# The second MLP's sample product by seven quadrant products, chunks 1 to 14, and retention states loaded in the other parity

## The reference

```
h = _rms_norm(x, norm_mlp[i]) * (1.0 + sc2) + sh2
x = x + g2 * (jnp.square(jax.nn.relu(h @ mlp_w1[i])) @ mlp_w2[i])
```

## Time and profile before

| | us |
|---|---|
| median of 3 runs | 2645.57 |
| lowest and highest run | 2644.88, 2650.03 |
| profiled execution | 2645.16 |
| its span | 2643.4 |
| TensorE (matmul) busy | 2561.9 (97%) |
| VectorE busy | 1351.4 (51%) |
| ScalarE busy | 593.9 (22%) |
| GpSimd busy | 544.8 (21%) |

### The profile page before, as it was taken

The page is one execution under the profiler, slowest core; times in us unless marked ns, Lnnn a source line. Parts: engine busy times, 40 slices in busy tenths (PEclk is TensorE's granted clock), DMA queues, the critical chain, the costliest instruction groups (busy, mean ns, idle before and its releaser), DMA issues.

```text
span 2643.4 us, 37530 instructions
## 1 busy us (share of the span) xinstructions
PE 2561.9 (97%) x14604; PEld 2240.7 (85%) x14604; DVE 1351.4 (51%) x2366; ACT 593.9 (22%) x982; POOL 544.8 (21%) x230
## 2 busy tenths in 40 slices
PE   7899999979999999999999999999999999999998
PEld 3878899977888888888888888888888888888887
DVE  6635752264385556554556555564444444444445
ACT  3311122142231111111111112751112111121112
POOL 6124321162121212111112111011121211212110
PEclk9999999989999999999999999899999999999999
DMA  7314523274212211211211211011010100101102
GB/s 236 149 67 142 166 96 112 95 265 168 72 33 80 71 56 56 95 56 56 71 56 56 95 56 32 25 32 33 32 48 32 48 32 32 48 32 48 32 32 80
DMA packets 126263, 199.48 MB, mean 75 GB/s; under 512 B 4420, under 2 KB 102504, under 8 KB 125800
## 3 DMA queue, kind: packets, MB, share of 16 engines
q1 hardware_dynamic: 123216, 188.76, 21.1%
q10 hardware_dynamic: 2968, 9.63, 1.2%
HBM read 167.44 MB, written 26.74 MB: 73 GB/s over the span
## 4 chain that ended last, share of the span: by engine, by line
PE 88%; DVE 5%; issue 2%; DMA 2%; ACT 2%; POOL 1%; ACTq 0%; SPq 0%; DVEq 0%; POOLq 0%
PE bank L314 83%; PE bank L1404 1%; PE bank L1432 1%; PE bank L1557 1%; DMA ada_st_in<-in_ada_w_dram 1%; PE bank L1469 1%; DVE ada_acc_in L1053 0%; PE bank L1735 0%; DVE vtok L1107 0%; DMA SB<-state_spill 0%; DVE xgm L1220 0%; POOL ringL L854 0%; DVE h1L L1227 0%; DVE X L1061 0%; ACT pF L736 0%
## 5 line engine op out<-in xcount | busy, mean ns | idle before, releaser
L854 POOL TENSOR_TENSOR ringL<-stage,ringH 128x2048 fp32r<-128x2048 f32 x82 | 392.8, 4790 | 1823.1 <-ACT ringH L532 1823.1
L1061 DVE SCALAR_TENSOR_TENSOR X<-bank,mod,X 128x512 f32<-128x512 f32 (+1 forms) x792 | 515.1, 660 | 363.4 <-PE bank L314 359.1
L314 PE MATMUL bank<-midH,ringH 128*128 128x512 f32 (+1 forms) x1536 | 546.7, 356 | 3.3 <-DVE X L1061 3.3
L314 PE MATMUL bank<-midL,ringH 128*128 128x512 f32 (+1 forms) x1536 | 544.9, 355 | 0.0
L314 PE MATMUL bank<-midH,ringL 128*128 128x512 f32 (+1 forms) x1536 | 544.7, 355 | 0.0
L314 PE MATMUL bank<-hH,ringH 128*128 128x512 f32 (+1 forms) x1248 | 447.2, 358 | 0.2 <-DVE hL L1227 0.2
L314 PE MATMUL bank<-hH,ringL 128*128 128x512 f32 (+1 forms) x1248 | 442.5, 355 | 0.0
L314 PE MATMUL bank<-hL,ringH 128*128 128x512 f32 (+1 forms) x1248 | 442.4, 355 | 0.0
L1336 DVE TENSOR_TENSOR relu<-relu 128x512 f32<-128x512 f32 (+1 forms) x192 | 146.3, 763 | 568.9 <-ACT relu L774 568.8
L774 ACT ACTIVATE relu<-bank 128x512 f32<-128x512 f32 (+1 forms) x192 | 100.9, 527 | 1375.9 <-PE bank L314 1375.9
L314 PEld LDWEIGHTS bank<-midH,ringH 128*128 128x128 f32 x1536 | 291.5, 190 | 46.1 <-DVE X L1061 6.5
(11 more groups left out here) (191 smaller groups left out, 2888.1 us busy)
## 6 DMA issues: line engine op xcount, KB each, us to landing
stage<-in_mlp_w_dram SPq DMA_DIRECT2D x64, 1024.0 KB, 5.3
ada_st_mlp<-in_ada_w_dram SPq DMA_DIRECT2D x18, 1536.0 KB, 8.3
stage<-in_ev_w_in_dram SPq DMA_DIRECT2D x14, 1024.0 KB, 5.1
ada_st_in<-in_ada_w_dram SPq DMA_DIRECT2D x8, 1536.0 KB, 9.5
ada<-in_ada_w_dram SPq DMA_DIRECT2D x8, 1024.0 KB, 13.3
x_spill<-X SPq DMA_DIRECT2D x1, 5120.0 KB, 18.5
gate_spill<-gate_st ACTq DMA_DIRECT2D x8, 640.0 KB, 3.7
gt<-gate_spill SPq DMA_DIRECT2D x20, 256.0 KB, 3.3
```

Of the source, the lines that this page charges most:

```text
L314: mm = nc.tensor.matmul(out, a, b, start=first and n == 0, stop=last and n == 2)
L854: nc.gpsimd.tensor_tensor(ringL[slot][:, :], stage[:, :], ringH[slot][:, :].bitcast(F32), ALU.subtract).then_inc(w_lo, 1)
L1061: V.scalar_tensor_tensor(out=X[:, d, cols(t)], in0=src[:, 0:TB[t][1]], scalar=gate_ap, in1=X[:, d, cols(t)], op0=ALU.mult, op1=ALU.add).th ...
```

## The change

In the second MLP the chunks 1 to 14 run a new function `mlp_fast` on each engine. The prompt's block keeps its products. The sample tokens' second product is cut into two halves of the output (four tiles each), two halves of the hidden units (one tile each) and two blocks of tokens, and the eight quadrant products are replaced by seven (Winograd's form of Strassen's scheme). Four of them use a sum of weight quadrants (S1 to S4, made by GpSimd in float32, split as the units are) or a sum of hidden quadrants (T1 to T4, made by VectorE). A quadrant product is four products of three matmuls, one for each output tile, and each is evicted on its own. Some add to a bank that was evicted before and holds its value (`CHAIN`).

The order on TensorE: first products 0, 1, 2; the quadrants 1 and 2 (8 products); first products 3, 4, 5; the quadrants 6, 5, 7, 3, 4, two output tiles at a time (20 products); 8 products of the prompt. The squares of the first products 3 to 5 go to ScalarE. The lowerings of the prompt's two hidden tiles (`p0`, `p1`) stand on VectorE behind the evictions of products 11 and 13.

```diff
+FAST_SEQ = ([(1, d) for d in range(HD)] + [(2, d) for d in range(HD)]
+            + [(p, d) for d0 in range(0, HD, 2) for p in (6, 5, 7, 3, 4) for d in (d0, d0 + 1)] + [("prompt", d) for d in range(DT)])
+FAST_BANK = [(2, 3, 6, 1, 4, 5, 2, 3)[d] if p == "prompt" else (6, 1)[d % 2] if p in (2, 3, 5) else 2 + d for p, d in FAST_SEQ]
...
+            def second_product(n):
+                own = earlier(FAST_BANK, n)
+                pe.wait_ge(m2_ev[l], p0 + own + 1)
+                pe.wait_ge(mid_lo[l], h0 + LO_ORDER.index(m_name) + 1)
...
+                pair_pass(bank[FAST_BANK[n]][:, :], wH, wL, mH, mL, p not in CHAIN, True, chained=True).then_inc(m2_mm[l], 1)
```

VectorE's part:

```diff
+            square(0)
+            lower("B11", b11)
...
+            square(1)
+            lower("B21", b21)
+            square(2)
+            dve.wait_ge(sqr_ok[l], n0 + 3)
+            V.tensor_tensor(t1, b12, b11, ALU.subtract).then_inc(t_full[l], 1)
+            for n in range(2 * HD):
+                evict(n)
...
+            V.tensor_tensor(t2, b22, t1, ALU.subtract).then_inc(t_full[l], 1)
+            V.tensor_tensor(t3, b22, b12, ALU.subtract).then_inc(t_full[l], 1)
+            dve.wait_ge(t_full[l], 4 * ch - 2)
+            V.tensor_tensor(t4, b21, t2, ALU.subtract).then_inc(t_full[l], 1)
+            lower("T1")
+            dve.wait_ge(t_full[l], 4 * ch)
+            lower("T2")
+            lower("T3")
+            lower("B22")
+            lower("T4")
+            for n in range(2 * HD, FAST_GRP):
+                evict(n)
+                if n in (11, 13):
+                    lower("p0" if n == 11 else "p1")
```

The end of ScalarE's part, and GpSimd's:

```diff
+            relu(5, hidden("p1")[2])
+            square(5, hidden("p1")[2])
+            act.wait_ge(sqr_ok[l], n0 + 6)
+            high("p1")
+            split_hi(U + 2, (m1_mm[l], n0 + PAIRS), U_MLP[l] % 2)
...
+            nc.gpsimd.tensor_tensor(s1, a21, a22, ALU.add).then_inc(s_add[l], 1)
+            nc.gpsimd.tensor_tensor(s3, a11, a21, ALU.subtract).then_inc(s_add[l], 1)
...
+            split_lo(U + 1, (U_MLP[l] + 1) % 2)
+            pool.wait_ge(s_hi[l], ch)
+            pool.wait_ge(t_full[l], 4 * ch - 3)
+            nc.gpsimd.tensor_tensor(sumL[:, :, :], sumF[:, :, :], sumH[:, :, :].bitcast(F32), ALU.subtract).then_inc(s_lo[l], 1)
+            split_lo(U + 2, U_MLP[l] % 2)
```

The states of block `k` go to `S[d][(k + 1) % 2]`, so that the first load does not overwrite the final states; SP's wait for the input products moves behind the loads:

```diff
-        sp.wait_ge(in_mm, IN_CUM[N_IN])
...
-                sp.dma_start(S[d][k % 2][:, :, :].rearrange("p h e -> p (h e)"), s_dram[d][k]).then_inc(s_back[k % 2], 16)
+                sp.dma_start(S[d][(k + 1) % 2][:, :, :].rearrange("p h e -> p (h e)"), s_dram[d][k]).then_inc(s_back[k % 2], 16)
...
         state_loads(0)
+        for d in range(2):
+            sp.dma_start(new_state[0, 0, d].rearrange("h d e -> d h e"), S[d][NT % 2][:, :, :]).then_inc(new_out, 16)
+        sp.wait_ge(new_out, 32)
         state_loads(1)
```

More of the change, by code:

```diff
@@ L112, in advances_before @@
     return sum(1 for a in ADVANCE if a < s)
+END_NEED = [products(1, NCH - 1) + DT * (1 + (0 if n >= NS else 1 + n // 4)) for n in END_TILES]
 def after(eng, sem, n):
@@ L221, in build @@
     ones = small("ones", [P, P])
-    r_b = [at(f"relu{i}", A_V + 2 * i, [P, 512]) for i in range(3)]
+    r_b = [at(f"relu{i}", A_AD + 3 + 2 * i, [P, 512]) for i in range(3)]
     acc = at("acc", A_E + 15, [P, T])
@@ L305, in cols, with pair_pass @@
         return slice(t0, t0 + w)
-    def pair_pass(out, w_hi_ap, w_lo_ap, m_hi_ap, m_lo_ap, first, last, weights_moving=False):
+    def pair_pass(out, w_hi_ap, w_lo_ap, m_hi_ap, m_lo_ap, first, last, weights_moving=False, chained=False):
         if weights_moving:
@@ L313, in pair_pass @@
         for n, (a, b) in enumerate(terms):
-            mm = nc.tensor.matmul(out, a, b, start=first and n == 0, stop=last and n == 2)
+            mm = nc.tensor.matmul(out, a, b, start=first and n == 0, stop=last and n == 2, skip_group_check=chained)
         return mm
@@ L938, in mlp @@
             split_lo(U_MLP[l] + 2 * ch + 1, (U_MLP[l] + 1) % 2)
+            if l == 0 and last:
+                band_tables()
             if not (l == 1 and last):
                 split_lo(U_MLP[l] + 2 * ch + 2, U_MLP[l] % 2)
-        mlp(0, 0, first=True)
[L942 to L950, removed]
@@ L1357, in mlp, with mlp_fast, square, lower @@
                         finish(j)
+        def mlp_fast(l, ch):
+            n0, h0, p0 = PAIRS * ch, halves(l, ch), products(l, ch)
+            def square(g):
+                dve.wait_ge(relu_ok[l], n0 + g + 1)
+                V.tensor_tensor(r_b[g][:, :], r_b[g][:, :], r_b[g][:, :], ALU.mult).then_inc(sqr_ok[l], 1)
+            def lower(name, src=None):
+                hi, lo, full = hidden(name)
+                dve.wait_ge(mid_hi[l], h0 + LO_ORDER.index(name) + 1)
+                V.tensor_tensor(lo, full if src is None else src, hi.bitcast(F32), ALU.subtract).then_inc(mid_lo[l], 1)
+            def evict(n):
+                t, d = FAST_TILE[n]
+                own = earlier(FAST_TILE, n)
+                update(m2_mm[l], p0 + n + 1, m2_ev[l], bank[FAST_BANK[n]], mod[:, l, 5 * DT + d, TB[t][2]:TB[t][2] + 1], t, d,
+                       (m2_ev[l], p0 + own + 1))
+            def ada(part):
+                if l == 0:
+                    ada_part(BATCHES_L0 + ch, 1, part, 4)
+            b11, b21, b12 = (r[:, :] for r in r_b)
+            t1, t2, t3, t4, b22 = (hidden(name)[2] for name in ("T1", "T2", "T3", "T4", "B22"))
+            ada(0)
+            square(0)
+            lower("B11", b11)
+            ada(1)
+            square(1)
[5 more added lines that the diff above has]
+                evict(n)
+            ada(2)
+            ada(3)
+            dve.wait_ge(sqr_ok[l], n0 + 4)
+            dve.wait_ge(t_full[l], 4 * ch - 3)
+            V.tensor_tensor(t2, b22, t1, ALU.subtract).then_inc(t_full[l], 1)
[12 more added lines that the diff above has]
+                    lower("p0" if n == 11 else "p1")
         mlp(0, 0, first=True)
@@ L1658, in mlp @@
                     g = HT * nth + f
-                    after(pe, relu_ok[l], g - 3 if first else n0 + g - 1)
+                    after(pe, relu_ok[l], g - 3 if first else n0 + (max(g - 1, 0) if last else g - 1))
+                    if last and g == 1:
+                        pe.wait_ge(m2_ev[l], products(l, ch))
                     if first and g == HT:
```

242 lines of the change are left out of this document (194 added, 48 removed).

## The result

| | before | after |
|---|---|---|
| median of 4 runs each, same chip | 2645.49 us | 2705.50 us |
| lowest, highest | 2644.88, 2650.03 | 2702.20, 2707.02 |
| profiled execution (its span) | 2645.16 (2643.4) | 2706.0 (2704.3) |

The change makes the kernel slower: 1.0221 times the time before, 95% interval 1.0204 to 1.0239, though TensorE issues 168 matmuls fewer. The forecast was 2698.

What follows compares the result with a forecast made beforehand. TensorE's unbroken matmuls were taken as the bound. A chunk: -2.72 + 1.6 + 3.5 + 1.5 = +3.9 us, in 14 chunks +54.6; 2645.16 + 54.6 - 2.5 = 2697, given as 2698 us with an odd clock fall; range 2625 to 2712.

Steps and rivals of the forecast that it cites:

- The removed work: Sample tokens' second product, seven quadrants for eight: 12 matmuls of 512 columns less, 2.72 us saved a chunk.
- The first place: Seventh quadrant product: TensorE waits for a bank that the fifth's eviction must free; 1.6 us a chunk, ends 0 and 2.2.
- The second place: Prompt lowerings among the last twenty products: GpSimd's low half holds p0, TensorE stands 3.5 us a chunk; bounds 0 to 4.6.
- B: End of the sixth first product in a chunk, the moment from which the steps to the p0 lowering were timed.
- the 0.2 us at later products: Extra TensorE wait a few products after the 3.5 us stand, VectorE still behind; taken as swallowed by the half clock.
- The clock: After the 3.5 us stand, matmuls run some 3 us at half clock: 1.5 us lost a chunk, ends 0 and 3.
- The states: Retention stage: state loads issued earlier, so TensorE's first product starts sooner; 2.5 us gained, ends 0 and 3.6.
- GpSimd's tables: Moved from first to last chunk of the first MLP, into GpSimd's idle time: cost 0, at worst 1 us.
- all hidden: Rival: neither place costs anything, only the matmul saving and the states' gain count; 2605 us, chance 0.06.
- nothing meets GpSimd: Rival: no lowering is held, second place and clock cost vanish, first place stays; 2627 us, chance 0.15.
- GpSimd comes second: Rival: p0 goes first and GpSimd holds p1, +1.7 us a chunk, no stand over 2 us; 2666 us, chance 0.15.
- the stand without the clock: Rival: both stands occur but the clock does not fall, +2.6 us a chunk; 2679 us, chance 0.15.

Runs made afterwards that it cites:

- the first three experiments: Changed kernel with GpSimd waiting for both prompt lowerings (2626.81 us), with those lowerings moved ahead of GpSimd (2625.05), with GpSimd waiting for p0 only (2670.34).
- the filled kernel: Changed kernel plus 15 unused 512-column matmuls a chunk, into unused bank 7 ahead of the 17th quadrant product: 2679.02 us.
- the kernel with four banks: Changed kernel with banks 6, 1, 7, 0 for quadrant 2 in place of 6 and 1 twice, and first products 3 and 5 moved: 2678.19 us.
- the kernel with both places mended: Changed kernel with GpSimd waiting for both prompt lowerings and with four banks for quadrant 2: 2603.87 us.
- the first experiment: Changed kernel with one wait more: GpSimd starts the next unit's low half only when p0 and p1 are lowered; 2626.81 us.

## Why the prediction was right

**The removed work.** -2.72 us a chunk; the kernel in which GpSimd waits has 54.00, and without its first stand (below, 1.63) that is 2.71 under the 55.08 of before. It could be read off because one unbroken chain of matmuls says that a removed one counts in full.

**The first place.** Predicted 1.6, measured 2054.49 - 2052.75 - 0.23 = 1.51, in every chunk. The second matmul behind such a stand starts 0.34 us after the first in place of 0.23, so the price is 1.63 in the kernel where GpSimd waits (2033.36 less 2031.61, then 2033.70). The four banks gave back only 54.00 - 52.65 = 1.35, because they bring the pause of 0.26.

**The second place.** With B = 2067.22 the steps were: GpSimd's low half at B + 3.36, measured B + 3.38; the lowering at B + 3.68, measured B + 3.62; its end at B + 8.25, measured B + 8.20; the stand 3.5, measured 2076.22 - 2072.47 - 0.23 = 3.52. The point that carried the sign, a lowering held like the square of the earlier trace rows although its two inputs are different tiles, was shown by the first three experiments. The Trainium skill (SBUF — State Buffer, Who interferes with whom) has that rule, and the trace agrees: 4.58 us beside GpSimd, 0.41 without it. Evictions ran on, as the earlier trace rows had it: two took 1.40 us from 2003.61 on, with GpSimd at work from 2003.85. In the filled kernel the whole place costs 57.87 - 54.00 = 3.87 us, 0.35 over the stand. Of the 0.2 us at later products that the prediction names, one shows there: a matmul six products later starts 0.34 us after its forerunner, 0.11 late; the matmul behind the stand is 0.10 late, and the rest of the 0.35 is not accounted for.

**The clock: the term that was mis-sized.** "I take 1.5 us a chunk": it is 1.86 by the filled kernel and 1.4 in the kernel with four banks. In that step I gave every fall the 3 us at half clock that the earlier trace rows have after 1619.77. The stretches show that the fall comes at another moment of the stand from chunk to chunk: where it comes early, 5.5 us of work run at half clock (2015.94 to some 2021.4: 0.64 over two us is 1.44 at half), where it comes late 3.3 (2076.22 to some 2079.5). Half of these times is 2.7 and 1.6 us; the two chunks are 2.40 and 1.35 us longer than the filled kernel's 57.87. What makes up the 0.3 us between is not shown; work that would have waited for VectorE in any case is a guess. In the kernel with four banks, which has no first stand some 20 us earlier, no chunk had the long one: its thirteen falls last 3.4 us each, where in the kernel after 3.4 and 6.8 us alternate through all fourteen chunks.

| us a chunk | predicted | measured | from |
|---|---|---|---|
| fewer matmuls | -2.72 | -2.71 | 54.00 - 1.63 - 55.08 |
| first place | +1.6 | +1.63 | the stand and the matmul behind it, GpSimd waiting |
| second place | +3.5 | +3.87 | 57.87 - 54.00 (with the later products) |
| clock | +1.5 | +1.86 | 59.73 - 57.87 |
| sum | +3.9 | +4.65 | 59.73 - 55.08 |

The chunk of the four-bank kernel in which the clock did not fall checks this: 55.08 - 2.71 + 0.26 + 3.87 = 56.50, as measured. That the prediction took 55.21 for the chunk before changes nothing in its sum, which counts differences alone.

**The states.** Predicted -2.5, measured -3.0 in the kernel after and -2.8 alone. The load of a state is no longer what comes last at the first product, which is 3.8 us earlier from the stage's start; 3.0 are left at its end, and states still end waits there, of up to 2.84 us at 584.67 (5.86 before).

**GpSimd's tables** at nothing: from GpSimd's last low half ahead of them to the matmul behind the stand of 2.26 us it is 82.49 us in both kernels (1537.28 to 1619.77, 1533.67 to 1616.16).

**The sum.** Fourteen times 4.65 is 65.1, and the MLP's 65.2 are all in these chunks. 2645.16 + 65.2 - 4.4 = 2706.0. The chunks cost 10.6 us more than the 54.6 of the forecast, nearly all of it by the clock (14 x 0.36 = 5.0) and the second place (14 x 0.37 = 5.2); what lies ahead of the MLP gave 1.9 us more than the 2.5, and 1 us had been put on top. So the forecast is 7.5 under the measured median because these two terms were too small, and a little luck ahead of the MLP hides some of that. The rivals: *all hidden* is what the kernel with both places mended does (2603.87 against 2605), *nothing meets GpSimd* what the first experiment does (2626.81 against 2627), *GpSimd comes second* 2670 against 2666, and *the stand without the clock* 2679.02 against 2679. Each mechanism exists. Some of the closeness is chance: the filled kernel's chunk costs 57.87 - 55.08 = 2.79 us where that rival had 2.6, and 3.3 us were won ahead of its MLP where it had 2.5. Which mechanism the change gets is decided by 0.24 us between GpSimd's start and the lowering's.

**Open.** Why the fall of the clock comes early and late in turn, and once not at all, was not tried. The 0.7 us behind the first MLP are of the size of what differs from run to run.

## What to carry to other kernels

Before matmuls are taken out of a loop that TensorE bounds, write down when each helper's instruction starts in the shorter loop: here 2.7 us a chunk were earned and 7.4 lost, by one lowering 0.24 us behind a GpSimd instruction and by two banks too few. An instruction of VectorE with both inputs in SBUF that sits between evictions is kept away from GpSimd's long reads, by its place or by letting GpSimd wait; the two gave 3.0 and 2.9% here. A stand of some 3.5 us is counted with the stretch at half clock behind it, another 1.4 to 1.9 us here, although in one chunk the clock did not fall.

## What the runs showed of the hardware that was not expected

- With four banks, one stand of 3.37 us of idle time left the granted clock at 1.00, and the one 56.50 us later (the same instructions) was followed by 0.50. In the kernel after, the length at half clock alternated between some 3.4 and 6.8 us, the longer in part inside the stand.
- More matmuls, less time: 210 unused products made the kernel after 26.5 us faster, with the granted clock at 1.00 over the place where it had been 0.50.
- The matmul right behind one that had to wait was late too, by 0.11 us, at the first place of each kernel that keeps the two banks (0.34 us from start to start in place of 0.23).
